# Last combine straight after the last down products, overflow items as nested conditions, final norm in halves

## The reference

```
y_rows  = (silu(xb @ w_gate[e]) * (xb @ w_up[e])) @ w_down[e]     # rows of expert e
contrib = y_rows[pos] * gates[:, None]
x       = x + segment_sum(contrib, flat_tok)                      # each token gets its 2 experts' rows
out     = x * rsqrt(mean(x * x, axis=-1) + EPS) * norm_final_g    # 256 x 1024
```

## Time and profile before

| | |
|---|---|
| median of three runs | 1543.22 us |
| profiled execution | 1542.4 us, span 1540.6 us |
| TensorE busy | 1464.1 us of the span (95%) |
| granted TensorE clock, mean | 0.979 |
| last down product's ScalarE copy ends | 1512.16 us |
| last combine starts | 1524.80 us |
| first add of its result | 1530.03 us |
| last normed rows written | 1537.55 us |

### The profile page before, as it was taken

One profiled execution on the slowest core, in us unless ns is written; L12 is line 12 of the kernel. 1 busy time (PEld: TensorE's weight loads), 2 busy tenths in 40 slices (PEclk: granted clock), 3 DMA queues, 4 the chain that ended last, 5 costly groups with the idle time before them and its releaser, 6 DMA issues.

```text
span 1540.6 us, 34120 instructions
## 1 busy us (share of the span) xinstructions
PE 1464.1 (95%) x15645; PEld 897.5 (58%) x15645; DVE 413.6 (27%) x640; ACT 328.4 (21%) x477; POOL 28.6 (2%) x43
## 2 busy tenths in 40 slices
PE   4999899999999976999999999999999999999993
PEld 3986899999799964345345345345344354354352
DVE  3454554444565764110110100100100100000101
ACT  4332544334548732100000000000000000000001
POOL 1000000000001101000000000000000000000000
PEclk9998999999999998999999999999999999999997
DMA  9530455555454317899999999999999999999950
GB/s 301 176 110 28 151 192 185 176 186 191 137 157 135 134 55 299 293 391 420 363 398 414 376 393 405 379 396 399 385 396 391 392 402 389 388 405 382 383 206 30
DMA packets 132570, 438.53 MB, mean 285 GB/s; under 512 B 10602, under 2 KB 63936, under 8 KB 116032
## 3 DMA queue, kind: packets, MB, share of 16 engines
q1 hardware_dynamic: 131232, 432.73, 74.6%
q0 software_dynamic: 1184, 3.50, 0.8%
HBM read 435.15 MB, written 1.05 MB: 283 GB/s over the span
## 4 chain that ended last, share of the span: by engine, by line
PE 92%; DVE 3%; ACT 2%; issue 2%; DMA 1%; SPq 1%; POOL 0%; DVEq 0%; ACTq 0%
PE bank L1161 38%; PE bank L1182 19%; PE bank L790 9%; PE bank L791 9%; PE bank L792 9%; PE bank L1224 2%; ACT high L618 1%; PE bank L1206 1%; PE bank L890 1%; DMA raw<-in_ev_w_in 1%; DVE low L623 1%; PE bank L1197 0%; SPq L731 0%; PE bank L909 0%; PE bank L908 0%
## 5 line engine op out<-in xcount | busy, mean ns | idle before, releaser
L1161 PE MATMUL bank<-ring,arena 128*32 128x512 f32 (+1 forms) x6144 | 585.2, 540 | 0.0
L1161 PEld LDWEIGHTS bank<-ring,arena 128*32 128x32 f32 x6144 | 196.4, 110 | 364.5 <-issue 363.3
L1182 PE MATMUL bank<-ring,arena 128*32 128x256 f32 x5376 | 291.5, 379 | 0.0
L1182 PEld LDWEIGHTS bank<-ring,arena 128*32 128x32 f32 x5376 | 174.7, 110 | 117.1 <-issue 3.1
L623 DVE TENSOR_TENSOR low<-raw,high 128x2048 fp32r<-128x2048 f32 x74 | 169.2, 2290 | 174.2 <-ACT high L618 174.2
L790 PE MATMUL bank<-ht_h,high 128*128 128x256 f32 x672 | 193.0, 287 | 3.3 <-DVE vec L1661 3.0
L791 PE MATMUL bank<-ht_l,high 128*128 128x256 f32 x672 | 191.7, 285 | 0.0
L792 PE MATMUL bank<-ht_h,low 128*128 128x256 f32 x672 | 191.6, 285 | 0.0
L618 ACT ACTIVATE high<-raw 128x2048 fp32r<-128x2048 f32 x74 | 141.5, 1913 | 164.3 <-PE bank L792 160.0
L1988 DVE TENSOR_TENSOR expert_rows<-expert_rows,bank 128x512 f32<-128x512 f32 (+1 forms) x48 | 29.7, 620 | 472.6 <-PE bank L1161 253.7
L790 PEld LDWEIGHTS bank<-ht_h,high 128*128 128x128 f32 x672 | 130.5, 194 | 5.1 <-issue 4.6
(11 more groups left out here) (274 smaller groups left out, 1017.2 us busy)
## 6 DMA issues: line engine op xcount, KB each, us to landing
ring<-in_moe_w_down SPq DMA_DIRECT2D x112, 1024.0 KB, 8.0
ring<-in_moe_w_gate SPq DMA_DIRECT2D x64, 1024.0 KB, 9.4
ring<-in_moe_w_up SPq DMA_DIRECT2D x64, 1024.0 KB, 8.8
ring<-in_moe_w_gate SPq DMA_DIRECT2D x64, 768.0 KB, 5.9
ring<-in_moe_w_up SPq DMA_DIRECT2D x64, 768.0 KB, 6.5
raw<-in_ffn_w_gate SPq DMA_DIRECT2D x14, 1024.0 KB, 5.0
raw<-in_ffn_w_up SPq DMA_DIRECT2D x14, 1024.0 KB, 5.0
raw<-in_ffn_w_down SPq DMA_DIRECT2D x14, 1024.0 KB, 4.9
```

What stands on the lines that cost most here:

```text
L1161: ins = mm(ps(use)[q * GRP:(q + 1) * GRP, 0:width], rows[:, k, r * GRP:(r + 1) * GRP], weights[:, q, :, :], start=k == 0, stop=k == DK - 1)
L1182: ins = mm(ps(use)[q * GRP:(q + 1) * GRP, 0:DN], m_act_t[:, r, first + c, :], ring[:, at + c * DM + q * DN:at + c * DM + (q + 1) * DN], st ...
```

## The change

The last item of the eight gets its combine directly behind its last down product on TensorE, after the register load; each overflow item that runs then makes its own combine at its end. The loops on TensorE, ScalarE and VectorE, and the row of conditions on SyncE, become conditions nested in one another, with each item's number a constant, so that the five bodies are written out. VectorE adds the last contributions by token tile and column quarter (eight instructions of 128x256 in place of four of 128x512) and signals each column half of 512 through `x_final`; the memset and `experts_done` go. ScalarE squares by column halves, VectorE writes `hn` by column halves, and SyncE stores four pieces of 256 KB in place of two of 512 KB. VectorE makes all eight adds before the first norm factor.

```diff
--- before.py
+++ after.py
@@ -555,7 +555,7 @@
         rsel_ready = sem("rsel_ready")
         route_ready = sem("route_ready")
         sel_ready = sem("sel_ready")
-        experts_done = sem("experts_done")
+        x_final = sem("x_final")
         out_ready = sem("out_ready")
         out_done = sem("out_done")
 
@@ -756,14 +756,22 @@
             sp.wait_ge(route_ready, 1)
             n_items = sp.value_load(route_i[0:1, 0:1], min_val=NE, max_val=NITEM)
             extra = [sp.value_load(route_i[0:1, 1 + j:2 + j], min_val=0, max_val=NE - 1) for j in range(NOVER)]
-            for over in range(NOVER):
-                with sp.If(n_items > NE + over):
-                    first_turn(extra[over], NE + over - 1)
-                    later_turns(NE + over, extra[over])
+
+            def extra_items(over):
+
+                if over < NOVER:
+                    with sp.If(n_items > NE + over):
+                        first_turn(extra[over], NE + over - 1)
+                        later_turns(NE + over, extra[over])
+                        extra_items(over + 1)
+
+            extra_items(0)
             for t in range(T):
-                sp.wait_ge(out_ready, t + 1)
-                sp.dma_start(out_d[0, t * P:(t + 1) * P, :], hn[:, t, :]).then_inc(out_done, 16)
-            sp.wait_ge(out_done, 16 * T)
+                for half in range(2):
+                    cols = slice(half * 512, half * 512 + 512)
+                    sp.wait_ge(out_ready, 2 * t + half + 1)
+                    sp.dma_start(out_d[0, t * P:(t + 1) * P, cols], hn[:, t, cols]).then_inc(out_done, 16)
+            sp.wait_ge(out_done, 16 * 2 * T)
 
 
         @block.tensor
@@ -1151,7 +1159,7 @@
                 width = WIDTHS[part]
                 at = PLACES[j][1]
                 weights = ring[:, at:at + NQ * width].rearrange("p (b q i) -> p q b i", q=NQ, i=GRP)
-                rows = xg_all[:, item, :, :] if isinstance(item, int) else xg
+                rows = xg_all[:, item, :, :] if item < NE else xg
                 pe.wait_ge(*expert_landed(j, item))
                 for r in range(NG):
                     use = ("m" + kind, part, r)
@@ -1244,7 +1252,7 @@
                         expert_gate_up(j, item)
                     if first and j < DK:
                         gather(1, j)
-                    if key == ("g", 0, 1) and not first:
+                    if key == ("g", 0, 1) and 0 < item < NE:
                         combine(item - 1)
                     if key == ("u", 0, 0):
                         pe.wait_ge(sel_ready, item + 1)
@@ -1279,11 +1287,18 @@
                 expert_item(item)
             pe.wait_ge(route_ready, 1)
             n_items = pe.value_load(route_i[0:1, 0:1], min_val=NE, max_val=NITEM)
-            with pe.Fori(NE, NITEM) as item:
-                with pe.If(n_items > item):
-                    gather_extra(item)
-                    expert_item(item)
-            combine(n_items - 1)
+            combine(NE - 1)
+
+            def extra_items(item):
+
+                if item < NITEM:
+                    with pe.If(n_items > item):
+                        gather_extra(item)
+                        expert_item(item)
+                        combine(item)
+                        extra_items(item + 1)
+
+            extra_items(NE)
 
 
         @block.scalar
@@ -1307,11 +1322,14 @@
                     fn(unread[:, :], inv_ms[:, j - 1, :], ACT.Sqrt)
 
                 for t in range(T):
-                    if added is None:
+                    if j == 0:
                         fn(hn[:, t, :], x[:, t, :], ACT.Square, accum_out=ssq[:, j, t, 0:1]).then_inc(ssq_ready, 1)
                     else:
                         for half in range(2):
-                            act.wait_ge(*drained(added + (2 * t + half,)))
+                            if added is None:
+                                act.wait_ge(x_final, 2 * t + half + 1)
+                            else:
+                                act.wait_ge(*drained(added + (2 * t + half,)))
                             cols = slice(half * 512, half * 512 + 512)
                             fn(hn[:, t, cols], x[:, t, cols], ACT.Square,
                                accum_out=ssq[:, j, t, half:half + 1]).then_inc(ssq_ready, 1)
@@ -1505,11 +1523,16 @@
                 expert_item(item, item == 0)
             act.wait_ge(route_ready, 1)
             n_items = act.value_load(route_i[0:1, 0:1], min_val=NE, max_val=NITEM)
-            with act.Fori(NE, NITEM) as item:
-                with act.If(n_items > item):
-                    expert_item(item)
+
+            def extra_items(item):
+
+                if item < NITEM:
+                    with act.If(n_items > item):
+                        expert_item(item)
+                        extra_items(item + 1)
+
+            extra_items(NE)
             fn(unread[:, :], inv_ms[:, 3, :], ACT.Sqrt)
-            act.wait_ge(experts_done, 1)
             squares(4)
 
 
@@ -1574,7 +1597,7 @@
 
             def norm_factor(j, t):
 
-                if j in (0, 4):
+                if j == 0:
                     dve.wait_ge(ssq_ready, SQUARES_BEFORE[j] + t + 1)
                     steps.done(V.tensor_scalar(inv_ms[:, j, t:t + 1], ssq[:, j, t, 0:1], DM * EPS, None, ALU.add))
                 else:
@@ -2021,19 +2044,40 @@
             for item in range(NE):
                 expert_item(item, item == 0)
             n_items = dve.value_load(route_i[0:1, 0:1], min_val=NE, max_val=NITEM)
-            with dve.Fori(NE, NITEM) as item:
-                with dve.If(n_items > item):
-                    rows_extra(item)
-                    expert_item(item)
-            add_contributions(n_items - 1)
-            V.memset(r_max, 0.0).then_inc(experts_done, 1)
-
-
+
+            def extra_items(item):
+
+                if item < NITEM:
+                    with dve.If(n_items > item):
+                        rows_extra(item)
+                        expert_item(item)
+                        extra_items(item + 1)
+
+            def last_contributions(t):
+
+                for q in range(NQ):
+                    use = ("mc", q)
+                    if t == 0:
+                        dve.wait_ge(*filled(use, n_items - 1))
+                    cols = x[:, t, q * DN:(q + 1) * DN]
+                    ins = V.tensor_tensor(cols, cols, ps(use)[:, t * DN:(t + 1) * DN], ALU.add)
+                    if q % 2:
+                        ins.then_inc(x_final, 1)
+
+            def final_rows(t):
+
+                norm_factor(4, t)
+                for half in range(2):
+                    cols = slice(half * 512, half * 512 + 512)
+                    V.scalar_tensor_tensor(hn[:, t, cols], x[:, t, cols], rstd[:, 4, t:t + 1], g_row[:, cols],
+                                           ALU.mult, ALU.mult).then_inc(out_ready, 1)
+
+            extra_items(NE)
             dve.wait_ge(g_loaded, 16 * 5)
             for t in range(T):
-                norm_factor(4, t)
-                V.scalar_tensor_tensor(hn[:, t, :], x[:, t, :], rstd[:, 4, t:t + 1], g_row[:, :], ALU.mult,
-                                       ALU.mult).then_inc(out_ready, 1)
+                last_contributions(t)
+            for t in range(T):
+                final_rows(t)
 
 
 _WEIGHTS = ["norm_mix_g", "norm_ffn_g", "norm_final_g", "ev_w_in", "ev_b_forget", "ev_pool_w", "ev_pool_scale",
```

## The result

The changed kernel takes 1526.57 us (median of four runs, 1522.94 to 1527.02) where the kernel before takes 1542.9 (four runs, 1540.04 to 1543.8). The ratio is 0.9896, 95% interval 0.9872 to 0.9919: 16.3 us, about 1%, faster. Forecast were 1527.4 us and a range of 1524.0 to 1531.5. The profiled execution took 1527.02 us with a span of 1524.8.

The account below looks back on a forecast made before the run. TensorE bounds the expert stage, which stays; the tail after ScalarE's last copy, mostly issue at skips, shrinks from 28.4 to 0.3 + 2.95 + 7.0 + 2.75 = 13.0 us, 15.4 saved: 1527.4 us, range 1524 to 1531.5.

Parts of the forecast that it names:

- Part 1, the start: TensorE's last combine starts 0.3 us after ScalarE's last copy instead of 12.64, ahead of the skips: 12.34 us saved.
- Part 1, the combine: Last combine runs at the high clock, 2.95 us to the first add instead of 5.23: 2.28 us saved.
- Parts 2 and 3: Last adds, squares and norm: first add to last normed rows takes 7.0 us instead of 7.52, 0.5 saved.
- Part 4: Final stores in four pieces: last rows to the end takes 2.75 us instead of 3.05, 0.3 saved.
- Part 5: Remaining skips on all four engines stay hidden; ScalarE, with least cover, is ready some 1.6 us early.
- rival (a): ScalarE's skip over five bodies is long, 3.3 or 6.08 us: 1528.1 or 1530.9 us; chance 0.13.
- Rival (b): Combine still late, TensorE's sequencer stalling for instructions behind the register load: 5.4 us lost, 1532.8 us; chance 0.05.
- Rival (c): TensorE's skip over five items becomes the end, 30.4 us: 1547.8 us, slower than before; chance 0.02.
- The four terms: Tail pieces after the change: start 0.3, combine 2.95, adds and norm 7.0, stores 2.75 us.

Follow-up runs that it names:

- The late signal: Changed kernel, but the last combine also waits for ten small ScalarE copies behind its last copy of the down products; one run, 1533.81 us.
- 52 calls: Kernel before with 52 small products added at the head of TensorE's program, 208 instructions more; 1545.84 us beside 1546.22 before.

## Why the prediction was right

*Part 1, the start.* Right, and to a tenth: 12.34 us forecast, 12.43 measured. The moved combine alone shows that the place is the cause, and the nested conditions alone that the number of skips is not enough. The register load and its checks had ended by 1511.4, under the last products, as its row had it before.

*Part 1, the combine.* 2.28 forecast, 2.37 measured, 2.86 us from start to add. The sequencer's feed does not limit here: the 2.89 of the earlier trace rows holds with an empty queue too. It can behind a skip, as the pause of 1.03 us with the nested conditions alone shows. The late signal, in one run, shows the clock as the cause of 2.07 us.

*Parts 2 and 3.* 0.5 forecast, 0.78 measured. The mechanism is as told: tile 0's squares end at 1517.77, the factor starts at 1518.25 behind the adds. The terms were a little long: the adds took 2.73 us instead of 2.8, the factor started 0.07 us before their end instead of 0.03 after it, and the factor of tile 1 followed 2.00 us after that of tile 0 instead of 2.05. At tile 1 the two candidates lie close: the rows of tile 0 end at 1520.33, the squares of tile 1 at 1520.11, and the factor starts at 1520.25. By the chain of waits the rows end last, not the squares: two squares back to back took 1.32 us, not the 2 x 0.73 that I had put together. The register arithmetic between adds, for which I kept 0.8 us, cost nothing that can be seen in 2.73.

*Part 4.* The step that was sized worst: 0.3 forecast, 0.58 measured, landing 2.0 us instead of 2.3. I had stayed near the row of 512 KB; whole stores give back 2.6 and 3.08. The Trainium skill, "DMA: Bandwidth & Descriptors", section "Anatomy of one DMA", fits a DMA of the GpSimd path with 2.0 us plus the bytes over 436 GB/s. The estimate from it, 0.6 us less for half the bytes, is what the runs show. The level is not: by the fit 256 KB would take 2.6 us, and these stores, issued by SyncE, land in 2.0.

*Part 5 and the rivals.* ScalarE's skip over five bodies took 0.045 us and its table load began at 1513.06, so rival (a) did not come about. The 3.3 us that it took as SyncE's price of a jump were a mean of unequal steps: the branch rows start at 1479.5, 1484.6, 1486.6, 1489.8 and 1492.7 and last 0.045 to 0.055 us each, and what fills the time between them is open. Rival (b) neither: the combine started 0.21 us after the copy. Rival (c) neither: one jump over five items took 3.88 us, over one item 3.38 before. In the other kernels it was 3.45 to 3.78 over five items and 3.42 to 4.02 over one. Distance does not price a skip here. But the reading of the earlier trace rows was too simple: it took the two long skips as what the first two cost anywhere. The loop moved by 104 or 208 instructions has only one. Some 6 us of the tail before (6.05 and 5.66 by these two runs) were thus owed to where its loop happened to stand, and a moved combine is free of that. The Trainium skill, "Runtime: NRT & Kernel Launch", "Instruction fetch mechanics", has the instructions fetched in blocks and a taken branch outside the blocks held waiting for a fetch. That fits with four things here: skips of 0.22 and of 3.4 to 6.8 us with nothing between, a pause of 1.03 us in the middle of straight code behind a skip, the change of pattern with the shift, and five packets of the queue named "instruction" where there are two long skips and two where there is one. Which blocks were held at the second skip was not measured, so fetching as the cause of the long skips is argued, not shown.

*The sum.* The four terms missed by 0.09, 0.09, 0.26 and 0.28 us, all on the same side, 0.7 in total; the time came 0.8 below the forecast. That the whole time fits as well as the terms is in part luck: the four runs lie 4.1 us apart, and what differs there lies ahead of the tail (last section).

## What to carry to other kernels

Work on the critical path does not belong behind a run-time branch over a long body: put what is known to be needed ahead of the branch, and look into the sequencer's rows when a chain says "issue". A skip behind the last work cost nothing here as long as it ended before the last store did; nesting it was then worth nothing (tails of 13.63 and 13.80 us). An idle stretch of 7 to 13 us was paid twice on TensorE, once as idle time and once as a lower clock under the work that followed (4.62 to 5.23 us instead of 2.86).

## What the runs showed that was not expected

The same loop, skipped the same five times, takes 12.9 us before (1511.2 to 1524.1, from its first branch to its last) and 6.8 us (1511.4 to 1518.2) with 104 instructions more at the other end of the program.

From the ranking products near 594 us to the end of ScalarE's last copy the executions agree within 0.15 us: 594.1 to 1512.16 before, 594.5 to 1512.52 after, 590.7 to 1508.67 with the moved combine, 603.8 to 1521.75 with 52 calls. All that makes these runs differ by several us lies ahead. Part of it is there early: the first factor of the second norm, which no edit but the shifts comes near, is at 164.4 before, 162.0 after, and 158.9 with the halves alone. Another part comes in the second mixer: the stretch from there to the first factor of the fourth norm takes 408.7 us before and 411.3 after (573.1 and 573.3), 411.1 with the halves alone (570.0). Why it differs is open. For a change of 1 us at the end the tail tells more than the time of the whole.

```profile
L1582 DVE TENSOR_SCALAR inv_ms<-ssq x2: 213/214/214, 164.4 to 169.7; 128x1 f32<-128x1 f32 x2
```

Above the kernel before, below the one with the halves alone (durations in ns, first and last start):

```profile
L1586 DVE TENSOR_SCALAR inv_ms<-ssq x2: 214/214/214, 158.9 to 164.3; 128x1 f32<-128x1 f32 x2
```
